# Output banks of the softmax maps: one or two, and panels of the last layers in three banks or two

## The reference, cut to what matters

```
s = einsum(q, k) * scale (+ masks)      # 128 queries at a time
p = softmax(s)
o = einsum(p, v)                        # 128 x 64 for one head and one block of queries
```

```
q  = rope(h @ w_q)                      # 4 panels of 128 columns
xbc = silu(causal_conv4(h @ w_xbc))     # 12 panels
g_att = h @ w_g                         # 4 panels
```

## Time and profile before

| | us |
|---|---|
| median of 3 runs | 2446.85 (2446.08 to 2449.55) |
| the profiled execution, its time | 2448.79 |
| its span, first to last instruction | 2447.0 |
| TensorE / VectorE / ScalarE / GpSimd busy, share of the span | 97% / 58% / 42% / 11% |

### The profile page before, as it was taken

One profiled execution on the slowest core, in us unless ns is written; L12 is line 12 of the kernel. 1 busy time (PEld: TensorE's weight loads), 2 busy tenths in 40 slices (PEclk: granted clock), 3 DMA queues, 4 the chain that ended last, 5 costly groups with the idle time before them and its releaser, 6 DMA issues.

```text
span 2447.0 us, 32007 instructions
## 1 busy us (share of the span) xinstructions
PE 2374.6 (97%) x12074; PEld 1923.7 (79%) x12086; DVE 1424.7 (58%) x2366; ACT 1019.2 (42%) x1732; POOL 273.9 (11%) x260
## 2 busy tenths in 40 slices
PE   8999899999999999999999999989999998999998
PEld 7877788888887888788888866767888776678887
DVE  3545665655655666566556469947533578666333
ACT  3666664322334444443233344444422354444323
POOL 0000111000001000100000236302100233111001
PEclk8999999999999999999999999999999999999999
DMA  4311002333432111133433312111222221102321
GB/s 180 111 54 44 1 19 104 143 133 129 143 133 87 63 59 61 53 121 129 151 125 136 117 66 70 61 35 36 95 96 97 83 70 61 44 27 75 107 95 52
DMA packets 58039, 211.77 MB, mean 87 GB/s; under 512 B 6432, under 2 KB 6560, under 8 KB 57888
## 3 DMA queue, kind: packets, MB, share of 16 engines
q1 hardware_dynamic: 57456, 208.86, 24.9%
q10 hardware_dynamic: 432, 0.85, 0.1%
HBM read 207.60 MB, written 2.10 MB: 86 GB/s over the span
## 4 chain that ended last, share of the span: by engine, by line
PE 83%; DVE 7%; issue 4%; ACT 4%; POOL 1%; DMA 0%; SPq 0%; ACTq 0%; DVEq 0%; POOLq 0%
PE bank L459 76%; PE last_bank L459 4%; PE bank L469 3%; DVE arena L1146 1%; DVE arena L2233 1%; DVE arena L2235 1%; DVE small L832 1%; ACT wparts L567 1%; ACT arena L820 1%; POOL rstd L626 0%; DMA cb_sb<-cb_dram 0%; DVE arena L2568 0%; DVE wparts L571 0%; ACT arena L2141 0%; DVE arena_r L585 0%
## 5 line engine op out<-in xcount | busy, mean ns | idle before, releaser
L459 PE MATMUL bank<-hT,wparts 128*128 128x512 f32 x5520 | 1334.3, 398 | 6.0 <-DMA cb_sb<-cb_dram 3.5
L459 PEld LDWEIGHTS bank<-hT,wparts 128*128 128x128 f32 x5520 | 1033.6, 190 | 237.4 <-issue 23.2
L571 DVE TENSOR_TENSOR wparts<-ring,wparts 128x1024 fp32r<-128x1024 f32 x290 | 367.3, 1267 | 422.1 <-ACT wparts L567 421.7
L459 PE MATMUL bank<-arena_r,wparts 128*128 128x512 f32 x2400 | 550.5, 390 | 0.0
L459 PEld LDWEIGHTS bank<-arena_r,wparts 128*128 128x128 f32 x2400 | 449.4, 188 | 93.8 <-DVE arena_r L601 0.8
L567 ACT ACTIVATE wparts<-ring 128x1024 fp32r<-128x1024 f32 x332 | 348.2, 1049 | 157.6 <-PE bank L459 124.1
L820 ACT ACTIVATE arena<-bank,small 128x128 f32<-128x128 f32 (+3 forms) x192 | 100.9, 526 | 143.6 <-DVE small L832 142.4
L469 PE MATMUL bank<-cf_sb,arena 128*128 128x128 f32 (+1 forms) x816 | 130.3, 276 | 15.3 <-DMA cf_sb<-cf_dram 5.4
L459 PE MATMUL last_bank<-arena 128*128 128x64 f32 x972 | 131.4, 271 | 9.6 <-DVE arena L855 4.3
L459 PEld LDWEIGHTS last_bank<-arena 128*128 128x128 f32 x972 | 122.4, 192 | 18.8 <-issue 12.6
L832 DVE TENSOR_REDUCE small<-bank 128x1 f32<-128x128 f32 (+3 forms) x192 | 93.4, 487 | 56.7 <-PE bank L459 45.1
(11 more groups left out here) (277 smaller groups left out, 2123.3 us busy)
## 6 DMA issues: line engine op xcount, KB each, us to landing
ring<-weights_dram SPq DMA_DIRECT2D x388, 512.0 KB, 3.4
arena<-x_dram SPq DMA_DIRECT2D x4, 512.0 KB, 6.3
out_dram<-arena SPq DMA_DIRECT2D x4, 512.0 KB, 4.0
rot<-rot_dram SPq DMA_DIRECT2D x1, 512.0 KB, 10.9
rot<-rot_dram ACTq DMA_DIRECT2D x1, 512.0 KB, 3.2
cf_sb<-cf_dram SPq DMA_DIRECT2D x1, 416.0 KB, 9.3
cb_sb<-cb_dram SPq DMA_DIRECT2D x1, 264.0 KB, 10.1
vecs<-vec_dram ACTq DMA_DIRECT2D x1, 258.5 KB, 6.3
```

The source lines that it names most:

```text
L459: i = pe.matmul(*args, **kw)
L571: eng.tensor_tensor(wparts[:, slot, 1, :, :], ring[:, p % RAW, :, :], wparts[:, slot, 0, :, :].bitcast(F32), ALU.subtract)\
```

## The change

It has three parts. The outputs of nsa and dsa maps alternate between bank 2 and bank 7. To free bank 2, the second pool of the compressed branch shrinks from banks 0, 1, 2 to 0, 1, and everything of strand 1 in the dsa stages (queries and their rotations, conv panels, nat, last, cb, bn, gates) shares banks 0 and 1. The maps of forgetting attention and the panels beside them keep their pools.

```
-        CMP_POOL = (NBANK,), (0, 1, 2)
+        CMP_POOL = (NBANK,), (0, 1)
...
         nsa = softmax_maps("nsa", maps, Pb, PT, lambda i: small_cols(32, i), lambda i: small_cols(36, i, 6),
-                           [dve_made["vsw", "turned", 1]], (3, 4, 5, 6), (NBANK,), dve_every=8, busy=5)
+                           [dve_made["vsw", "turned", 1]], (3, 4, 5, 6), (2, NBANK), dve_every=8, busy=5)
...
             dsa = softmax_maps(K + "dsa", maps, Pb, PT, lambda i: small_cols(32, i), lambda i: small_cols(36, i, 6),
-                               [dve_made[K + "v", "turned", 0], act_made[K + "k high"]], (3, 4, 5, 6), (NBANK,),
+                               [dve_made[K + "v", "turned", 0], act_made[K + "k high"]], (3, 4, 5, 6), (2, NBANK),
                                dve_every=DSA_EVERY, together=True)
...
-                bank = banks.take(pe, (K + "nat", 0), POOLS[0])
+                bank = banks.take(pe, (K + "nat", 0), POOLS[0][:2])
...
-                bank = banks.take(pe, (K + "last", 0), POOLS[0])
+                bank = banks.take(pe, (K + "last", 0), POOLS[0][:2])
...
-                    bank = banks.take(pe, (K + "cb", g), POOLS[0])
+                    bank = banks.take(pe, (K + "cb", g), POOLS[0][:2])
...
-                    bank = banks.take(pe, (K + "bn", g), POOLS[0])
+                    bank = banks.take(pe, (K + "bn", g), POOLS[0][:2])
...
-                        linear = pe_linear_steps(pe, K + "ga", n, hT, KD, None, POOLS[0])
+                        linear = pe_linear_steps(pe, K + "ga", n, hT, KD, None, POOLS[0][:2])
...
-            early, late = conv(CONVS[:EARLY], True, POOLS[0]), conv(CONVS[EARLY:], False, POOLS[0])
+            early, late = conv(CONVS[:EARLY], True, POOLS[0][:2]), conv(CONVS[EARLY:], False, POOLS[0][:2])
...
-            queries = project(later, None, rtmp, vt, ROPE32, pool=POOLS[0])
+            queries = project(later, None, rtmp, vt, ROPE32, pool=POOLS[0][:2])
```

## The result

The changed kernel takes 2474.64 us (median of 4 runs, 2473.18 to 2476.97) against 2447.35 for the kernel before in the same session. The ratio is 1.0113 with a 95% interval of 1.010 to 1.0126: slower by 24 to 31 us, where 25 were forecast. The profiled execution has a span of 2471.6 us, 24.6 more than before.

A forecast was written before the change was run, and what follows sets the result against it. TensorE's stream of matmuls, busy 97% of the span, was taken as the bound; 32 us lost in the dsa stages, 4 gained in nsa and 3 in dsa outputs gave +25, so 2472 us, range 2456 to 2486 (chance 0.77).

The follow-up runs named there:

- e_panels: Kernel before with only the dsa panels, short steps and gates on banks 0 and 1, output pools unchanged; 2480.2 us against 2446.7.
- e_dsa: Kernel before with e_panels' change plus dsa outputs on banks 2 and 7, nsa stage unchanged; 2477.9 us against 2446.7.
- e_best_fill: Kernel before with nsa outputs alternating banks 7 and 2, dsa outputs likewise two banks from map 20, 12 useless matmuls before step last; 2438.8 us against 2446.1.

## What to carry to other kernels

Before a pool is made smaller, write down for each take which occupant it now follows: short steps that take every second turn of a pair turn it into a single bank for the long panels between them. Losses found by walking an engine's list aren't prices that can be added or taken out one by one, since a later wait for another engine's drain swallows what came before it. A second bank for outputs pays where it is free, and it should begin with the bank that nobody needs next.

## What the runs showed of the hardware

Which short wait is followed by half clock changed from one kernel to another at the same place. Behind the wait of 2.94 us conv 3's 24 matmuls took 7.36 us in e_panels and 5.74 in the changed kernel; behind that of 1.85 us conv 5's 18 took 4.39 and 5.98. In the nsa stage TensorE ran at granted clock 0.50 from 276 to 282 us in e_dsa and at 1.00 in before, with the same program up to there. The stretch costs some 1.6 us (103.7 against 102.1). The kernel before has such stretches of its own in both dsa stages, so a difference of 2 us between two single executions says nothing about an edit.

Much of the chance between executions is clock. The first nsa scores come at 243.8 us in before and at 238.0 in e_best_fill; the mean granted clock of the first 60 us is 0.86 and 0.97 (0.91 in the changed kernel, with 240.9). And 25 executions of before in one session go from 2441.4 us at a mean clock of 0.994 to 2451.2 us at 0.987.
